# The opening of a fused block on one core: Pool makes the first two weight remainders, root and first tiles in PSUM, high-part products first, one more column product on VectorE

## The chip, the cores and the metric

One core of a Trainium2 chip runs the program; seven are idle. The metric is the device time of one execution in microseconds (us). The engines have names of two kinds: TensorE (PE in the profile; PEld is its weight load), VectorE (DVE), ScalarE (ACT), GpSimd (POOL, "Pool" in the text) and SyncE (SP), which here only issues DMAs.

## The reference, cut to what matters

The program computes a state-space mixer block with its MLP and then a gated linear attention block with its MLP, 512 tokens of 1024 features. Only the first lines of the first block are of concern here:

```
c_act = silu(c)
mod = (c_act @ w_ada + b_ada)            # shift1, scale1: 2 x 1024 of its values come first
u = rms_norm(x, ln1) * (1.0 + scale1) + shift1
proj = u @ w_in                          # dt columns, then B, C, xs, z ... of eight groups
dt = softplus(dt + dt_bias)
```

All of it is fp32. The kernel gets fp32 accuracy from three fp32r products for each matmul: weights and data are split into a rounded high part and a remainder, and it sums high x high, high weight x low data, and low weight x high data.

## The kernel before, in words

**Layout.** Data is held transposed: features on 128 partitions, 512 tokens along a row, eight tiles j = 0 to 7 for 1024 features. A weight unit is 128 output columns for all 1024 features: a 128x1024 tile `wraw`, of which ScalarE makes the rounded `whi` (hi_part, L416) and VectorE or Pool the remainder `wlo` (lo_part, L436). There are two raw slots and four split slots. The weight of dt has tiles of its own: `dw`, `dwh`, `dwl`.

**The opening.** The first 60 us hold what has no work beside it.
1. SP issues, in this order (L2680 to L2712): the parameters, x, the modulation weights' slab 0 (8 pieces), dw, weight units 0 and 1, slab 1, then it waits for remainder 0 (semaphore w_split), issues unit 2, slab 2, waits for remainder 1, issues unit 3, slab 3, and so on.
2. ScalarE squares the tiles of x (L2812), TensorE sums them with a matrix of ones into PSUM bank 6, ScalarE makes the root in `nrs` (Ln L548, Exp L550), then rounds dw into dwh (L2816).
3. The modulation comes in four chunks c, each for two tiles of u. VectorE multiplies the rows of a slab with c_act and adds them up, one operation for each of KD[c] pieces k (`columns`, L2994 and L2996, the sum is kept in PSUM bank 5; the last goes to `macc`). TensorE adds the remaining pieces itself (`direct`, L3242: eight minus KD[c] pieces) and sums macc over the partitions (`reduced`, L3249). VectorE then makes mod and g1s for two tiles (`modulation`, L3006 and L3008).
4. For each tile j of u: x times root (`scaled_a`: VectorE for tiles 0 and 1, L2971; Pool for 2 to 7, L2735), the rounded uhi (`rounded_a`, VectorE L2977, for tiles 0 and 2; ScalarE L2824 for the others), the full value on ScalarE (L2825, into two turns of `nsq`), and the low part ulo = full - uhi on VectorE (`low_a`, L2982). Semaphore "hi" counts full tiles, "u" counts low parts.
5. TensorE does 5 outputs (dt and weight units 0 to 3, banks 4, 0, 1, 2, 3) by 8 tiles by 3 products = 120 products (`first_units`; lines 1348 to 1350, called through `part`). The products of tile k wait for low part k, and each new output waits for its remainder (dw_lo, w_split).

**What sets the order.** Nothing but the order written for each engine, and semaphores between them: every engine works through its own list, and a wait at the head of it holds all behind. VectorE's list of the opening, before, is: columns of chunk 0, scaling 0, modulation 0, rounding 0, scaling 1, low 0, remainder dwl (L3018), remainder of unit 0, low 1, columns of chunk 1 (6), one of chunk 2, modulation 1, rounding 2, one column, low 2, one column, low 3, five columns, two of chunk 3, modulation 2, two, low 4, one, low 5, two, modulation 3, low 6, low 7. Pool's is: remainder of unit 1, scaling 2 and 3, remainder 2, remainder 3, scaling 4 to 7.

After the opening TensorE goes on with unit 4 (L450 to L452), the transposes of dt (they wait for the dt chain on VectorE and ScalarE) and the rest of the 280 units.

## Time and profile before

| | |
|---|---|
| median of 3 runs | 1746.01 us (1745.83 to 1746.41) |
| the profiled execution: time, span | 1746.1 us, 1744.4 us |
| mean granted TensorE clock | 0.997 |
| PE busy | 1722.9 us, 99% |
| PEld busy | 1457.2 us, 84% |
| DVE busy | 1203.4 us, 69% |
| ACT busy | 828.9 us, 48% |
| POOL busy | 312.8 us, 18% |

Shares of busy time are over the whole span, and the opening is a thirtieth of it. There the timelines have to be read: each gives the start of an instruction from the first instruction of the program, its length, engine, line, operation, output and input, and in brackets how long its engine had been idle before it and what ended that. The time of a run is some 1.7 us longer than the span. Matmul starts are spaced closer than their lengths, since they are pipelined: the distance of starts is what counts.

### The profile page before, as it was taken

The page shows a single profiled execution, that of the slowest core. Times are in us where ns is not written, and L with a number is a line of the kernel's source. Part 1 is how long each engine was busy: PE and PEld are TensorE (multiplying, and loading weights), DVE is VectorE, ACT ScalarE, POOL GpSimd, SP SyncE. Part 2 cuts the span into 40 slices and gives each one's busy share as a digit, 9 for nine tenths or more (in the row PEclk, how much of TensorE's full clock was granted, in tenths as well). Part 3 has the DMA queues.
Part 4 walks back from the last instruction along what each step waited for, and adds up shares of the span by engine and source line. Part 5 has one row for each costly group of instructions (what it writes and reads, how often), then busy time and mean ns, then how long its engine had stood idle before and what let it go on. Part 6 is the DMA issues. An engine that isn't in the chain of part 4 may idle for free.

```text
span 1744.4 us, 26127 instructions
## 1 busy us (share of the span) xinstructions
PE 1722.9 (99%) x9074; PEld 1457.2 (84%) x9074; DVE 1203.4 (69%) x1678; ACT 828.9 (48%) x1273; POOL 312.8 (18%) x370
## 2 busy tenths in 40 slices
PE   7999999999999999999999999999999999999998
PEld 4888888888888888888888888889998888999997
DVE  6788777775356665589855665776656788667764
ACT  4666666665322222355313543665544474444443
POOL 2111111110011110002111125221110112222212
PEclk9999999999999999999999999999999999999999
DMA  9343333332545563326555563111122414223221
GB/s 336 107 127 115 121 121 121 116 114 73 181 133 192 192 192 121 109 97 214 184 192 179 192 219 114 60 50 49 42 71 70 140 46 154 97 98 106 100 72 50
DMA packets 76245, 221.12 MB, mean 127 GB/s; under 512 B 9328, under 2 KB 19952, under 8 KB 76144
## 3 DMA queue, kind: packets, MB, share of 16 engines
q1 hardware_dynamic: 56944, 160.43, 27.6%
q0 software_dynamic: 17632, 56.83, 10.6%
q10 hardware_dynamic: 1568, 2.52, 0.5%
q8 instruction: 62, 1.02, 0.2%
q14 instruction: 39, 0.32, 0.1%
HBM read 217.52 MB, written 2.23 MB: 126 GB/s over the span
## 4 chain that ended last, share of the span: by engine, by line
PE 87%; DVE 6%; issue 3%; DVEq 2%; ACT 1%; DMA 1%; ACTq 0%; POOLq 0%; POOL 0%; SPq 0%
PE bank L450 16%; PE bank L451 16%; PE bank L452 16%; PE bank L1348 3%; PE bank L2412 3%; PE bank L2413 3%; PE bank L1349 3%; PE bank L1350 3%; PE bank L2414 3%; PE bank L2366 2%; PE bank L2368 2%; PE bank L2367 2%; PE bank L1401 1%; PE bank L1400 1%; PE bank L1399 1%
## 5 line engine op out<-in xcount | busy, mean ns | idle before, releaser
L436 DVE TENSOR_TENSOR wlo<-wraw,whi 128x1024 fp32r<-128x1024 f32 x246 | 311.6, 1268 | 125.5 <-ACT whi L416 104.9
L416 ACT ACTIVATE whi<-wraw 128x1024 fp32r<-128x1024 f32 x217 | 229.2, 1058 | 331.3 <-PE bank L452 216.2
L450 PE MATMUL bank<-uhi,whi 128*128 128x512 f32 x916 | 359.1, 392 | 0.2 <-DVE wlo L436 0.2
L452 PE MATMUL bank<-uhi,wlo 128*128 128x512 f32 x916 | 356.6, 389 | 0.0
L451 PE MATMUL bank<-ulo,whi 128*128 128x512 f32 x916 | 356.5, 389 | 0.0
L452 PEld LDWEIGHTS bank<-uhi,wlo 128*128 128x128 f32 x916 | 172.0, 188 | 36.1
L450 PEld LDWEIGHTS bank<-uhi,whi 128*128 128x128 f32 x916 | 172.0, 188 | 35.7 <-DVE wlo L436 0.6
L451 PEld LDWEIGHTS bank<-ulo,whi 128*128 128x128 f32 x916 | 172.0, 188 | 34.8
L1085 POOL DMA_DIRECT2D aring<-in_ada x160 | 86.0, 538 | 519.3 <-DVE aacc L1099 214.0
L450 PE MATMUL bank<-vhi,whi 128*128 128x512 f32 x408 | 159.5, 391 | 0.0
L452 PE MATMUL bank<-vhi,wlo 128*128 128x512 f32 x408 | 158.8, 389 | 0.0
L451 PE MATMUL bank<-vlo,whi 128*128 128x512 f32 x408 | 158.8, 389 | 0.0
L1099 DVE SCALAR_TENSOR_TENSOR aacc<-aring,c_act,aacc 128x512 f32 (+1 forms) x168 | 123.6, 750 | 11.4 <-issue 2.0
L2213 DVE TENSOR_TENSOR qlo<-qsrc,qhi 128x512 fp32r<-128x512 f32 x98 | 85.1, 890 | 45.4 <-ACT qhi L2207 33.3
L2412 PE MATMUL bank<-v2hi,whi 128*128 128x512 f32 x236 | 92.6, 392 | 0.0
L2413 PE MATMUL bank<-v2lo,whi 128*128 128x512 f32 x236 | 92.5, 392 | 0.0
L2414 PE MATMUL bank<-v2hi,wlo 128*128 128x512 f32 x236 | 91.8, 389 | 0.0
L450 PEld LDWEIGHTS bank<-vhi,whi 128*128 128x128 f32 x408 | 76.6, 188 | 16.3 <-DVE vlo L1212 0.3
L452 PEld LDWEIGHTS bank<-vhi,wlo 128*128 128x128 f32 x408 | 76.6, 188 | 16.0
L451 PEld LDWEIGHTS bank<-vlo,whi 128*128 128x128 f32 x408 | 76.6, 188 | 15.7
L1348 PE MATMUL bank<-uhi,whi 128*128 128x512 f32 x216 | 88.3, 409 | 0.0
L1350 PE MATMUL bank<-uhi,wlo 128*128 128x512 f32 x216 | 84.7, 392 | 0.0
(527 smaller groups left out, 3506.1 us busy)
## 6 DMA issues: line engine op xcount, KB each, us to landing
wraw<-in_units SPq DMA_DIRECT2D x252, 512.0 KB, 3.8
aring<-in_ada POOLq DMA_DIRECT2D x160, 256.0 KB, 3.5
qsrc<-in_units SPq DMA_DIRECT2D x28, 512.0 KB, 3.8
slab<-in_ada SPq DMA_DIRECT2D x32, 256.0 KB, 7.5
es<-decay_rows POOLq DMA_DIRECT2D x32, 256.0 KB, 4.6
eac<-decay_rows POOLq DMA_DIRECT2D x32, 128.0 KB, 2.9
x<-in_xT SPq DMA_DIRECT2D x4, 512.0 KB, 5.6
xr<-in_xT ACTq DMA_DIRECT2D x1, 2048.0 KB, 14.1
```

What stands on the lines that cost most here:

```text
L416: act.activation(whi[:, at % SLOTS, :], wraw[:, at % RAW, :], ACT.Copy).then_inc(w_hi, 1)
L436: dve.tensor_tensor(wlo[:, at % SLOTS, :], wraw[:, at % RAW, :], whi[:, at % SLOTS, :].bitcast(f32), ALU.subtract).then_inc(w_split, 1)
L450: pe.matmul(out, wh, rhs_hi(k), start=first and k == 0, stop=False)
L451: pe.matmul(out, wh, rhs_lo(k), start=False, stop=False)
L452: mm = pe.matmul(out, wl, rhs_hi(k), start=False, stop=last and k == KT - 1)
L1085: pool.dma_start(aring[:, n % ARING, :], src[k * P:(k + 1) * P, bass.ds(it * 512 + col0, 512)]).then_inc(N2[f"ada_ld{n % ARING}"], 16)
L1099: last = dve.scalar_tensor_tensor(acc, w, c, acc, ALU.mult, ALU.add)
L1348: pe.matmul(out, wh, rhs_hi(k), start=k == 0, stop=False)
L1350: mm = pe.matmul(out, wl, rhs_hi(k), start=False, stop=k == KT - 1)
L2412: pe.matmul(psum[i][:], whi[:, slot, s], v2hi[:, v + t, :], start=t == 0, stop=False)
L2413: pe.matmul(psum[i][:], whi[:, slot, s], v2lo[:, v + t, :], start=False, stop=False)
L2414: mm = pe.matmul(psum[i][:], wlo[:, slot, s], v2hi[:, v + t, :], start=False, stop=t == 3)
```

## The change: what it does

- **Pool** makes dwl and the remainders of units 0 and 1, ahead of its scalings; before, VectorE made the first two. Semaphores dw_hi and dw_lo become one, dw_split (1: dwh is there, 2: dwl too). Pool's scalings now also wait for dt_nega, which stands behind a second Exp.
- **Root in PSUM.** Ln goes to nrs, Exp to PSUM bank 6, from which VectorE scales tiles 0 and 1. Later, behind the copy of unit 1, ScalarE does the Exp once more, into nrs, for Pool's scalings.
- **Full tiles 0 and 1 in PSUM.** `full_a` gives banks 3 and 2, which units 3 and 2 use later; the other tiles stay in nsq.
- **KD** goes from [7, 6, 8, 7] to [7, 7, 8, 7]: chunk 1 has seven column products on VectorE and one piece on TensorE.
- **VectorE's order** of column products among low parts and modulations is another.
- **TensorE's order.** The first products wait for dwh and the rounded tile 0 (new semaphore u_first) and go out kind by kind: high x high, high weight x low data, remainder last. From tile 3 on the high and remainder products of a tile wait for the full tile ("hi"), and only the product with the low part waits for "u". `direct(1)` and `reduced(1)` come before anything of unit 2, `reduced(2)` among the products of unit 3, `reduced(3)` behind the first six products of tile 5.

```diff
-KD = [7, 6, 8, 7]
+KD = [7, 7, 8, 7]
...
+        def full_a(j):
+            return psum[3 - j][:] if j < 2 else nsq[:, j % 2, :]
...
-            pool.wait_ge(norm_sem["rs"], 1)
+            pool.wait_ge(S["dw_split"], 1)
+            pool.tensor_tensor(dwl[:], dw[:], dwh[:].bitcast(f32), ALU.subtract).then_inc(S["dw_split"], 1)
+            lo_part(pool, 0, 0)
+            lo_part(pool, 1, 0)
+            pool.wait_ge(S["dt_nega"], 1)
             pool.wait_ge(norm_sem["t"], 2)
-            pool.wait_ge(w_split, 1)
-            lo_part(pool, 1, 0)
             scaled_a(2)
             scaled_a(3)
             lo_part(pool, 2, 0)
...
-            norm_a.root(act, norm_a.bank)
+            act.activation(nrs[:], psum[6][:], ACT.Ln, scale=1.0 / D, bias=eps)
+            act.drain()
+            act.activation(psum[6][:], nrs[:], ACT.Exp, scale=-0.5).then_inc(norm_sem["rs"], 1)
             act.wait_ge(S["dw_ld"], 16)
-            act.activation(dwh[:], dw[:], ACT.Copy).then_inc(S["dw_hi"], 1)
+            act.activation(dwh[:], dw[:], ACT.Copy).then_inc(S["dw_split"], 1)
...
-                act.activation(nsq[:, j % 2, :], x0[:, j, :], ACT.Identity, scale=g1s[:, j:j + 1], bias=mod[:, j:j + 1]
+                act.activation(full_a(j), x0[:, j, :], ACT.Identity, scale=g1s[:, j:j + 1], bias=mod[:, j:j + 1]
                                ).then_inc(norm_sem["hi"], 1)
...
             hi_part(act, 1, 0)
+            act.activation(nrs[:], nrs[:], ACT.Exp, scale=-0.5)
             act.activation(nega[:], pc("a_log"), ACT.Exp).then_inc(S["dt_nega"], 1)
...
-                dve.tensor_tensor(x0[:, j, :], x0[:, j, :], nrs[:], ALU.mult).then_inc(norm_sem["t"], 1)
+                dve.tensor_tensor(x0[:, j, :], x0[:, j, :], psum[6][:], ALU.mult).then_inc(norm_sem["t"], 1)
...
-                dve.tensor_scalar(uhi[:, j, :], x0[:, j, :], g1s[:, j:j + 1], mod[:, j:j + 1], ALU.mult, ALU.add)
+                rounded = dve.tensor_scalar(uhi[:, j, :], x0[:, j, :], g1s[:, j:j + 1], mod[:, j:j + 1], ALU.mult, ALU.add)
+                if j == 0:
+                    rounded.then_inc(S["u_first"], 1)
...
-                dve.tensor_tensor(ulo[:, j, :], nsq[:, j % 2, :], uhi[:, j, :].bitcast(f32), ALU.subtract
+                dve.tensor_tensor(ulo[:, j, :], full_a(j), uhi[:, j, :].bitcast(f32), ALU.subtract
...
             low_a(0)
-            dve.wait_ge(S["dw_hi"], 1)
-            dve.tensor_tensor(dwl[:], dw[:], dwh[:].bitcast(f32), ALU.subtract).then_inc(S["dw_lo"], 1)
-            lo_part(dve, 0, 0)
+            columns(1, 0, 2)
             low_a(1)
-            columns(1, 0, KD[1])
-            columns(2, 0, 1)
+            columns(1, 2, KD[1])
             modulation(1)
             rounded_a(2)
-            columns(2, 1, 2)
             low_a(2)
-            columns(2, 2, 3)
+            columns(2, 0, 2)
             low_a(3)
-            columns(2, 3, KD[2])
-            columns(3, 0, 2)
+            columns(2, 2, KD[2])
+            columns(3, 0, 1)
             modulation(2)
-            columns(3, 2, 4)
+            columns(3, 1, 3)
             low_a(4)
-            columns(3, 4, 5)
+            columns(3, 3, 4)
             low_a(5)
-            columns(3, 5, KD[3])
+            columns(3, 4, KD[3])
...
+            def first_units(which, k):
+                pe.wait_ge(norm_sem["hi"], k + 1)
+                for n in which:
+                    product(n, k, "hi")
+                    product(n, k, "rest")
+                norm_a.ready(pe, k + 1)
+                for n in which:
+                    mm = product(n, k, "low")
...
+            pe.wait_ge(S["dw_split"], 1)
+            pe.wait_ge(S["u_first"], 1)
+            product(0, 0, "hi")
+            pe.wait_ge(w_hi, 1)
+            product(1, 0, "hi")
+            norm_a.ready(pe, 1)
+            products((0, 1), (0,), ("low",))
+            pe.wait_ge(norm_sem["hi"], 2)
+            products((0, 1), (1,), ("hi",))
+            pe.wait_ge(S["dw_split"], 2)
+            products((0,), (0, 1), ("rest",))
+            norm_a.ready(pe, 2)
+            products((0, 1), (1,), ("low",))
             pe.wait_ge(w_split, 1)
+            products((1,), (0, 1), ("rest",))
+            pe.wait_ge(w_hi, 2)
+            products((2,), (0, 1), ("hi", "low"))
             pe.wait_ge(w_split, 2)
+            products((2,), (0, 1), ("rest",))
             direct(1)
             reduced(1)
+            pe.wait_ge(w_hi, 3)
+            products((3,), (0, 1), ("hi", "low"))
+            norm_a.ready(pe, 3)
+            products((0, 1, 2), (2,), ("hi", "low", "rest"))
...
```

## Rows read from the trace of the kernel before

**Rows 1.** The page's chain that ended last: shares of the span by engine.
```profile
PE 87%; DVE 6%; issue 3%; DVEq 2%; ACT 1%; DMA 1%; ACTq 0%; POOLq 0%; POOL 0%; SPq 0%
```

**Rows 2.** Waits of TensorE, whole span: engine, line, releaser: total, times, longest.
```profile
PE bank L1348 <- DVE dwl L3018: 4.0, 1, 4.0
PE bank L1348 <- DVE ulo L2982: 1.2, 2, 0.6
```

**Rows 3.** Timeline of TensorE, opening: start, length, what, [idle before, releaser].
```profile
18.18 1.05 PE L3249 MATMUL bank<-con,macc 128*128 128x1 f32 x8
...
23.18 0.80 PE L1348 MATMUL bank<-uhi,dwh 128*128 128x512 f32 x1 [3.95 <-DVE dwl L3018]
...
28.44 1.84 PE L3242 MATMUL bank<-c_act,slab 128*128 128x1 f32 x16
30.14 1.03 PE L3249 MATMUL bank<-con,macc 128*128 128x1 f32 x8
...
34.22 0.50 PE L1348 MATMUL bank<-uhi,dwh 128*128 128x512 f32 x1 [0.60 <-DVE ulo L2982]
...
44.20 0.50 PE L1348 MATMUL bank<-uhi,dwh 128*128 128x512 f32 x1 [0.58 <-DVE ulo L2982]
...
47.74 0.95 PE L3242 MATMUL bank<-c_act,slab 128*128 128x1 f32 x8
...
59.79 0.39 PE L450 MATMUL bank<-uhi,whi 128*128 128x512 f32 x1
```

**Rows 4.** Timeline of VectorE, opening.
```profile
20.08 0.55 DVE L2977 TENSOR_SCALAR uhi<-x,g1s,mod 128x512 fp32r<-128x512 f32 x1
...
21.91 1.22 DVE L3018 TENSOR_TENSOR dwl<-dw,dwh 128x1024 fp32r<-128x1024 f32 x1
...
25.80 3.24 DVE L2996 SCALAR_TENSOR_TENSOR bank<-slab,c_act,bank 128x512 f32<-128x512 f32 x4
...
31.21 0.16 DVE L3006 TENSOR_TENSOR mod<-bank,par 128x4 f32<-128x4 f32 x1 [0.40 <-PE bank L3249]
31.45 0.47 DVE L3008 SCALAR_TENSOR_TENSOR g1s<-mod,par 128x2 f32<-128x2 f32 x1
...
41.33 0.16 DVE L3006 TENSOR_TENSOR mod<-bank,par 128x4 f32<-128x4 f32 x1
...
43.45 0.69 DVE L2982 TENSOR_TENSOR ulo<-nsq,uhi 128x512 fp32r<-128x512 f32 x1
...
44.89 1.17 DVE L2982 TENSOR_TENSOR ulo<-nsq,uhi 128x512 fp32r<-128x512 f32 x1
```

**Rows 5.** Timeline of ScalarE, opening.
```profile
18.85 1.04 ACT L2816 ACTIVATE dwh<-dw 128x1024 fp32r<-128x1024 f32 x1
...
23.10 1.04 ACT L416 ACTIVATE whi<-wraw 128x1024 fp32r<-128x1024 f32 x1
...
28.13 1.06 ACT L416 ACTIVATE whi<-wraw 128x1024 fp32r<-128x1024 f32 x1 [3.90 <-DMA wraw<-in_units]
...
42.62 0.80 ACT L2825 ACTIVATE nsq<-x,mod,g1s 128x512 f32<-128x512 f32 x1
```

**Rows 6.** Timeline of Pool, opening.
```profile
24.50 2.60 POOL L436 TENSOR_TENSOR wlo<-wraw,whi 128x1024 fp32r<-128x1024 f32 x1 [23.52 <-DVE wlo L436]
27.06 2.53 POOL L2735 TENSOR_TENSOR x<-x,nrs 128x512 f32<-128x512 f32 x2
29.54 2.37 POOL L436 TENSOR_TENSOR wlo<-wraw,whi 128x1024 fp32r<-128x1024 f32 x1
...
44.23 2.99 POOL L2735 TENSOR_TENSOR x<-x,nrs 128x512 f32<-128x512 f32 x2 [2.38 <-DVE ulo L2982]
```

**Rows 7.** Line 1534, VectorE copies beside Pool's products: ns min/median/max.
```profile
L1534 DVE COPY kdf<-ez x8: 294/673/1221, 1149.8 to 1272.7; 128x256 f32<-128x256 f32 x8
```

**Rows 8.** Timeline of SP's queue, opening.
```profile
24.29 0.34 SPq L2700 DMA_DIRECT2D wraw<-in_units  x1
```

**Rows 9.** Windows: stretch, busy of PE, PEld, DVE, ACT, POOL, granted clock, DMA.
```profile
20.00:22.00 2.00, 0.00 (x0) 0.00 (x0) 1.84 (x4) 1.98 (x3) 0.00 (x0) 0.50 1.09 351
...
26.00:28.00 2.00, 2.00 (x9) 1.57 (x8) 1.85 (x3) 0.00 (x0) 2.00 (x2) 0.79 1.00 354
```

51 lines of the change are left out of this document (27 added, 24 removed).

## The prediction, made before the change was timed

> **What bounds the kernel now.** I read the chain of waits first [rows 1]: 87% of it is TensorE, so the whole kernel ends when TensorE has done its matmuls. The waits of TensorE [rows 2] say where it is held up in the part that the change touches: 4.0 us for the first remainder (dwl), 1.2 us in two waits for the low parts of u. Then I put the timelines of the first 60 us side by side: TensorE [rows 3], VectorE [rows 4], ScalarE [rows 5], Pool [rows 6]. The reader is to see there that TensorE's first product starts at 23.18, that it waits again before 34.22 (u of tile 2) and before 44.20 (u of tile 4), and that from 44.20 it has no gap to 59.79, when the five opening accumulations are done. From 44.20 it does 60 products and two short stretches: 15 products in 47.74 - 44.20 = 3.54, so 0.236 each with restart, about 0.2275 in the flow. Nothing after 59.79 waits for long (the other waits of [rows 2] are elsewhere and small), so a shift of 59.79 goes into the end one to one. VectorE is the engine that sets 34.22 and 44.20: it is almost without idle time from 20 to 47, and the low parts stand between its column products.
>
> **The change, part by part.** The sum is made on the profiled execution: span 1744.4, its own time 1746.1, against a median of 1746.0; so a shift of the span is put straight on 1746.0.
>
> *Root and two full tiles in PSUM.* The Ln and Exp of the root and ScalarE's full tiles keep their length (0.80 to 0.81 a tile in [rows 5]; no row writes a 128x512 tile to PSUM, bounds 0.7 to 0.85; I take 0.80). ScalarE gets one more Exp (0.63 before, same row kind) after the second weight copy, in a stretch where it waits for a DMA until 28.13 [rows 5]: nothing. VectorE's two scalings and two subtractions take one operand from PSUM; the nearest rows are 0.69 and 0.75, I take 0.69.
>
> *Remainders to Pool.* VectorE loses dwl and wlo0: 1.22 each [rows 4], 2.3 us of its time at their spacing. Pool takes 2.37 for such an operation undisturbed [rows 6]. It starts when ScalarE has written dwh, 18.85 + 1.04 = 19.89 [rows 5], plus 0.08 to 0.17 (Pool starts 0.09 after the low part that ends at 44.14): 19.97 to 20.06. VectorE's rounding of tile 0 starts at 20.08 [rows 4]. This is the step on which I stake most. Pool and VectorE exclude each other for operations that use two SBUF reads: the g1s operation took 0.47 at 31.45 and ended with Pool's remainder (29.54 + 2.37 = 31.91), though the same form takes 0.16; the low part at 44.89 took 1.17 in place of 0.69 while Pool scaled [rows 4, 6]. Column products, with one operand in PSUM, ran beside Pool at full speed (3.24 for four from 25.80, with Pool busy since 24.50). The rounding reads one SBUF tensor, but takes 0.55 for 512 elements where a column product takes 0.75, so it seems to read by both ways, and a COPY with one SBUF source shows 0.29 at best and 0.67 in the median of eight, next to Pool's products [rows 7]. If it is excluded, it waits from 20.08 to about 0.15 before Pool's end at 22.34, and ends at 22.74 instead of 20.63. Bounds: 0 to 2.3 us; I take 2.1.
>
> On that point the Trainium skill is sharper than the rows. Its page "SBUF — State Buffer", section "SBUF: two separate sides", has the pair of ports shared by VectorE and GpSimd as an exclusive lock, for VectorE operations with two SBUF inputs or in a two-port mode; "VectorE: DVE Perf Modes", section "The perf-mode tier table (the rule you actually need)", puts an fp32 tensor_scalar from SBUF in such a mode. By these rules the rounding is held and the sum is the one below; without them for one-source operations it would be about 0 to +0.6. No row of this trace shows a TENSOR_SCALAR held by Pool.
>
> *What follows, in time.* PE: first product at 22.8 (before 23.18). Second scaling to 23.5, low part 0 to 24.1 (before 22.0). ScalarE waits for the scaling: uhi1, full tile 1 to 25.04, second weight copy to 26.0 (before 24.14 [rows 5]). Pool: wlo0 behind the rounding, 22.32 + 0.27 + 2.37 = 24.96; wlo1 26.08 to 28.45 (before 24.50 + 2.60 = 27.10 [rows 6]); tiles 2 and 3 scaled to 30.9 (2.53 for two; before 29.6); wlo2 30.9 to 33.26 (before 31.91). SP issues the third weight tile when wlo0 is written: at 24.98, before 24.29 [rows 8]; it landed 3.8 later and does so again, and all slabs behind it come 0.7 later. That is hidden: wlo2 waits for Pool, not for the tile, and the second slab is not read before 34.7.
>
> *KD 6 to 7 and the new places of column products.* One more product on VectorE, 0.83 at its spacing; TensorE's direct stretch halves, from 1.84 to 0.95 (its forms at 28.44 and 47.74 [rows 3]). Columns of chunk 1 now run from 24.0 to 30.45, with low part 1 between: 7 x 0.83 + 0.61. Before they ended at 29.9 (25.80 + 3.24, and one of 0.83 behind). TensorE: 18 products for outputs 0 to 2 by 29.2, direct 0.82 beside it, reduction 30.5 to 31.56, modulation(1) at 31.60 (before 31.21). g1s at 31.84 then waits for wlo2 until 33.2, rounding 2 at 33.4 (before right behind 31.92), low part 2 34.13 to 34.82 (before just ahead of 34.22). So u of tile 2 comes at 34.88 for TensorE, 0.66 late. VectorE's idle and held time here (1.1 before 31.60, 1.4 behind Pool) eats what it was relieved of; and of chunk 2 nothing is done, where two products had been done by then and a third was next.
>
> *Chunk 2 and 3.* From 34.7: two products, low part 3, six products, one of chunk 3: 9 x 0.83 + 0.7 = 8.2, to 43.0. modulation(2) at 43.14 (before 41.33 [rows 4]): 1.8 late. ScalarE's full tile 4 is written at 45.08 (before 42.62 + 0.80 = 43.42 [rows 5]).
>
> *High-part products first.* Before, tile 4 waited for its low part (44.14, start 44.20 [rows 3]). Now it starts on the full tile alone: 45.14. Of the 1.8 us the order gives back 0.8. TensorE has done its 38 other products, 38 x 0.2275 + 0.9 after 34.88, at 44.6 or so, so it waits 0.4 to 0.6 at that place as before. Tiles 5 to 7 have slack or lose about 0.15 (full tile 6 at 53.87 against TensorE at 53.8). Their 60 products and the two stretches are the same work: 45.14 + 15.6 + 0.15 = 60.9, against 59.79.
>
> The dt chain starts 1.5 later too, and TensorE gets to its transposes 1.1 later; before, it had about 1 us of slack there. Nothing is added.
>
> Sum: the end of the opening 1.1 us later, **1747.1**.
>
> **The rivals.**
> *A. VectorE gets in first at 20.08, or its rounding is not held.* For it: the two starts are only 0.02 to 0.11 apart. Then the first product is at 20.7, wlo0 25.2, wlo1 27.6, modulation(1) at 30.2. But the third tile lands at 29.0, its copy is ready at 30.1, and wlo2 starts at 30.3: g1s (30.4) is held to 32.5. u of tile 2 at 34.3, full tile 4 at 44.5: +0.5, 1746.5.
> *B. No operation of the opening is held twice* (Pool starts wlo2 after 30.7, or takes turns differently): low part 2 at 32.1, two us earlier than before, full tile 4 at 42.44, TensorE starts on it at 42.5 instead of 44.20, plus 0.2 lost in the thinner slack: -1.5, 1744.5. Against it: the held g1s and low part of [rows 4].
> *C. The clock falls again.* Slower than before: TensorE's clock was at the lower of its two levels (1.2 GHz, 0.50 in [rows 9]) from 20.0 to 26.8 after TensorE had only one-column matmuls (the last at 18.18 + 1.05 [rows 3]) and then none; it came back with TensorE busy since 23.18. In the forecast TensorE is idle from 32.4 to 34.9, in rival A from 31.1 to 34.3. Before, its gap there was 0.6. If this drops the clock for another 6.8 us while products are due, TensorE does half of what it would in them: 6.8 / 2 = 3.4 lost, less 0.6 of wait before tile 4: +2.8 on top, 1749.9. [...] Against it: the earlier fall followed a longer near-idle stretch.
> *D. The change does less than it says:* TensorE's early products, on half clock, win nothing because remainders and low part 2 end last anyway. That is inside the forecast and A.
>
> **How the numbers follow.** Forecast 0.45, A 0.25, B 0.13, C 0.12, other 0.05. The range has to reach B (1744.5) and most of C: 1744.2 to 1749.6; the likeliest's own range is 1746.3 to 1748.2 (the 0.15 and 0.08 us of each handover add up). A measurement of this kernel tells 0.2% from nothing, 3.5 us: faster than 1742.5 needs more than the stalls ahead of 34 and 44 (1.2) and the start won (2.5) without any loss, 0.03; slower than 1749.5 is half of C and a little, 0.07; within, 0.90.
>
> **What would show it.** Right: in the new timeline the rounding of tile 0 has some 2.6 us instead of 0.55 and ends 0.4 to 0.6 behind Pool's first remainder; g1s of chunk 1 is long and ends with Pool's wlo2; TensorE waits 2 to 3 us before the third output's tile 2 (34 to 35) and starts tile 4 at about 45. Wrong: a rounding of 0.55 beside a busy Pool; low part 2 before 33; TensorE free of gaps after 31; a granted clock of 0.50 after 30 (then C).

## The result and the profile after

The changed kernel takes **1748.71 us** (median of 22 runs, 1747.32 to 1750.33); the kernel before, on the same chips, 1746.32 (22 runs, 1745.13 to 1747.63). The ratio is 1.0014 [1.0009, 1.002]: 2.4 us slower, less than the 0.2% that the prediction took as no change, yet on the slower side of zero with its whole interval. The sign that was forecast is there, and so is the mechanism, on a neighbouring operation; +1.1 us was too little.

The profiled execution after has 1747.71 us, span 1746.0, mean clock 0.996. It is the third shortest of its kernel's 22: +1.6 against the profiled execution before, where the medians are +2.4 apart. The other 0.8 us can't be seen in this profile; only the times of the runs speak of them.

VectorE after, the lines that answer to [rows 4]:

```profile
19.69 2.28 DVE L3020 SCALAR_TENSOR_TENSOR g1s<-mod,par 128x2 f32<-128x2 f32 x1
22.07 0.55 DVE L2987 TENSOR_SCALAR uhi<-x,g1s,mod 128x512 fp32r<-128x512 f32 x1
...
32.39 0.16 DVE L3018 TENSOR_TENSOR mod<-bank,par 128x4 f32<-128x4 f32 x1 [1.97 <-PE bank L3257]
32.63 0.85 DVE L3020 SCALAR_TENSOR_TENSOR g1s<-mod,par 128x2 f32<-128x2 f32 x1
...
34.37 0.69 DVE L2994 TENSOR_TENSOR ulo<-nsq,uhi 128x512 fp32r<-128x512 f32 x1 [0.24 <-ACT nsq L2834]
...
43.46 0.16 DVE L3018 TENSOR_TENSOR mod<-bank,par 128x4 f32<-128x4 f32 x1 [0.29 <-PE bank L3257]
43.70 0.37 DVE L3020 SCALAR_TENSOR_TENSOR g1s<-mod,par 128x2 f32<-128x2 f32 x1
```

Pool after, for [rows 6]:

```profile
19.62 2.34 POOL L2741 TENSOR_TENSOR dwl<-dw,dwh 128x1024 fp32r<-128x1024 f32 x1 [18.64 <-ACT dwh L2825]
23.85 4.73 POOL L436 TENSOR_TENSOR wlo<-wraw,whi 128x1024 fp32r<-128x1024 f32 x2 [1.89 <-ACT whi L416]
28.54 2.52 POOL L2738 TENSOR_TENSOR x<-x,nrs 128x512 f32<-128x512 f32 x2
31.10 2.37 POOL L436 TENSOR_TENSOR wlo<-wraw,whi 128x1024 fp32r<-128x1024 f32 x1
...
41.52 2.54 POOL L2738 TENSOR_TENSOR x<-x,nrs 128x512 f32<-128x512 f32 x2
```

Pool's dwl runs from 19.62 to 21.96. In it stands an operation on two numbers a partition, g1s, that takes 0.16 us elsewhere: 2.28 us, to 21.97. The rounding behind it has its usual 0.55. The same again at 32.63, where g1s ends with Pool's remainder of unit 2 (31.10 + 2.37 = 33.47, g1s 33.48). A short one follows in chunk 2: g1s takes 0.37 at 43.70 and ends with Pool's scalings (41.52 + 2.54 = 44.06).

TensorE after, for [rows 3], and SP's queue, for [rows 8]:

```profile
22.76 0.77 PE L3268 MATMUL bank<-uhi,dwh 128*128 128x512 f32 x1 [3.35 <-DVE uhi L2987]
23.82 0.80 PE L3268 MATMUL bank<-uhi,whi 128*128 128x512 f32 x1 [0.30 <-ACT whi L416]
...
27.07 0.63 PE L3268 MATMUL bank<-ulo,dwh 128*128 128x512 f32 x1
27.50 0.63 PE L3268 MATMUL bank<-ulo,whi 128*128 128x512 f32 x1
...
31.32 1.03 PE L3257 MATMUL bank<-con,macc 128*128 128x1 f32 x8
...
35.12 0.50 PE L3268 MATMUL bank<-uhi,dwh 128*128 128x512 f32 x1 [1.73 <-DVE ulo L2994]
...
45.68 0.50 PE L3268 MATMUL bank<-uhi,dwh 128*128 128x512 f32 x1 [0.32 <-ACT nsq L2834]
...
61.55 0.39 PE L450 MATMUL bank<-uhi,whi 128*128 128x512 f32 x1
```

```profile
26.26 0.34 SPq L2703 DMA_DIRECT2D wraw<-in_units  x1
```

The opening ends at 61.55 instead of 59.79, +1.76, and the span is 1.6 longer. In this pair of executions what the opening loses arrives at the end; that it does so to a few tenths is not a rule, as the note below the table of the experiments shows. The waits of TensorE [rows 2] are now 3.4 us in one for the rounded tile 0 and 1.7 in one for low part 2.

The windows after, columns as in [rows 9]; the granted clock is the third number from the end:

```profile
20.00:22.00 2.00, 0.00 (x0) 0.00 (x0) 1.97 (x1) 0.00 (x0) 1.96 (x1) 0.50 1.09 353
...
26.00:28.00 2.00, 2.00 (x6) 1.51 (x6) 1.87 (x3) 0.74 (x3) 2.00 (x2) 0.50 0.42 113
28.00:30.00 2.00, 2.00 (x7) 1.61 (x6) 1.83 (x3) 0.04 (x1) 2.00 (x3) 0.61 0.91 312
30.00:32.00 2.00, 2.00 (x18) 1.88 (x17) 0.42 (x1) 1.02 (x1) 1.97 (x2) 1.00 0.98 331
```

The granted clock has two levels, 1.2 and 2.4 GHz (0.50 and 1.00). So a window of 2 us at 0.79 [rows 9] has 0.84 us at the lower one, and one at 0.61 has 1.56: the clock came back at 26.8 before and at 29.6 after. Until then products start 0.43 apart instead of 0.23 (27.07 to 27.50 above). From 26 to 28 TensorE has six records, where before it had nine. DMA has a hole there, 113 GB/s against 354: SP's queue has issued nothing since 20.4 and issues the third weight tile only at 26.26, behind the late remainder 0.

### The profile page after: what moved, and what is told of

The parts are those of the page before. It is cut to its first block, busy times and chain, and to the rows that moved or that the text cites. A ratio compares the mean times of both kernels' runs of the same rounds, so it can differ in the third digit from the quotient of the medians.

```text
span 1746.0 us, 26109 instructions
## 1 busy us (share of the span) xinstructions
PE 1723.7 (99%) x9066; PEld 1456.4 (83%) x9066; DVE 1204.1 (69%) x1677; ACT 829.5 (48%) x1274; POOL 316.5 (18%) x372
## 4 chain that ended last, share of the span: by engine, by line
PE 85%; DVE 6%; issue 3%; DVEq 2%; ACT 2%; DMA 1%; ACTq 0%; SPq 0%; POOLq 0%; POOL 0%
PE bank L450 16%; PE bank L452 16%; PE bank L451 16%; PE bank L2412 3%; PE bank L2413 3%; PE bank L2414 3%; PE bank L1348 2%; PE bank L1350 2%; PE bank L1349 2%; PE bank L2366 2%; PE bank L2368 2%; PE bank L2367 2%; PE bank L1401 1%; PE bank L1399 1%; PE bank L1400 1%
## 5 line engine op out<-in xcount | busy, mean ns | idle before, releaser
L450 PE MATMUL bank<-uhi,whi 128*128 128x512 f32 x916 | 359.1, 392 | 0.2 <-DVE wlo L436 0.2
L452 PE MATMUL bank<-uhi,wlo 128*128 128x512 f32 x916 | 356.6, 389 | 0.0
L1348 PE MATMUL bank<-uhi,whi 128*128 128x512 f32 x184 | 75.3, 409 | 0.0
L1350 PE MATMUL bank<-uhi,wlo 128*128 128x512 f32 x184 | 71.9, 391 | 0.0
```

What stands on the lines that cost most here:

```text
L450: pe.matmul(out, wh, rhs_hi(k), start=first and k == 0, stop=False)
L452: mm = pe.matmul(out, wl, rhs_hi(k), start=False, stop=last and k == KT - 1)
L1348: pe.matmul(out, wh, rhs_hi(k), start=k == 0, stop=False)
L1350: mm = pe.matmul(out, wl, rhs_hi(k), start=False, stop=k == KT - 1)
```

## The experiments

Each of the twelve kernels was run 11 times, the changed kernel 22 times, in turns with the kernel before on the same chip. *After* means the changed kernel. A "filler" is an extra matmul of dwh with itself into a bank whose content nobody reads; it leaves the output as it is.

| kernel | median | before | difference | ratio [95%] | opening ends* |
|---|---|---|---|---|---|
| after | 1748.71 | 1746.32 | +2.39 | 1.0014 [1.0009, 1.002] | 61.55 |
| 1 dwl behind rounding 0 | 1747.49 | 1745.90 | +1.59 | 1.0008 [0.9999, 1.0017] | 62.66 |
| 2 and wlo2 behind rounding 2 | 1747.86 | 1745.90 | +1.96 | 1.0011 [1.0002, 1.002] | 62.61 |
| 3 dwl, wlo0 on VectorE again | 1747.62 | 1745.90 | +1.72 | 1.0011 [1.0002, 1.002] | 60.45 |
| 4 after with fillers | 1746.77 | 1745.90 | +0.87 | 1.0002 [0.9993, 1.0011] | 61.57 |
| 5 no hold up to low part 2, fillers | 1746.14 | 1746.10 | +0.04 | 1.0001 [0.9992, 1.001] | 60.89 |
| 6 before with fillers | 1745.78 | 1746.10 | -0.32 | 1.0 [0.9991, 1.0009] | 60.23 |
| 7 as 3, fillers | 1746.53 | 1746.10 | +0.43 | 1.0004 [0.9995, 1.0013] | 59.98 |
| 8 as 4, KD[1] = 6 | 1747.61 | 1746.10 | +1.51 | 1.001 [1.0001, 1.0019] | 63.64 |
| 9 as 5, slabs loaded ahead | 1748.88 | 1746.68 | +2.20 | 1.0011 [1.0002, 1.002] | 61.98 |
| 10 as 9, two products ahead | 1748.46 | 1746.68 | +1.78 | 1.0012 [1.0003, 1.0021] | 61.76 |
| 11 before, high part first | 1746.51 | 1746.68 | -0.17 | 0.9999 [0.999, 1.0008] | 59.31 |
| 12 unit 0 first on Pool | 1745.45 | 1745.99 | -0.54 | 0.9997 [0.9988, 1.0006] | 59.05 |

*In the one profiled execution, whose time may lie up to 1.8 us off the median: the profiled ones of 5 and 8 are 0.9 and 1.7 above theirs, that of 3 is 1.8 below. Intervals are some 1.6 us wide to each side (1 us for the changed kernel's), so differences under that are read as hints, and the timelines carry the argument. The ratio is not the quotient of the two medians; for kernel 4 it stands for 0.3 us where the medians are 0.87 apart.

Three more things have to be known before single executions are compared.
- *They do not start alike.* The first modulation on VectorE starts at 19.59 before and 19.45 after, but at 19.94 in kernel 1, 19.84 in kernel 5, 18.98 in kernel 11 and 19.11 in kernel 12. The column "opening ends" holds these shifts of up to 0.6 us.
- *They do not end alike.* From the end of the opening to the end of the span it is 1684.6 us before and 1684.5 after, but 1683.5 in kernel 2 and 1685.5 in kernel 11. No opening explains that; it is as large as the whole effect, and its cause is open.
- *The clock.* In these profiles the lower level lasts, summed over the opening, 6.8 us before and in kernels 3 and 6, 10.2 in the changed kernel and in 1, 2, 8 and 11, 3.4 in 4, 7, 9 and 10, and nothing in 5 and 12. Behind the opening all have 1.00 up to the last few microseconds.

**1. Pool's dwl starts behind the rounding of tile 0.**

```diff
             pool.wait_ge(S["dw_split"], 1)
+            pool.wait_ge(S["u_first"], 1)
             pool.tensor_tensor(dwl[:], dw[:], dwh[:].bitcast(f32), ALU.subtract).then_inc(S["dw_split"], 1)
```

> The changed kernel, but Pool's first remainder also waits until VectorE has rounded tile 0 (so it starts some 0.9 us later and holds nothing of modulation 0). Before is 1746.3, the changed kernel 1748.7. Ports theory (Pool's remainders hold VectorE's modulation of chunks 0 and 1, each for 1 to 2 us, and that carries the loss): the g1s operation of chunk 0 falls from 2.28 to 0.16 us, the first product starts at about 20.6 instead of 22.76, the second hold stays or grows to 2 us because wlo2 now starts about when modulation 1 is ready; the end of the opening 0.8 to 1.3 us earlier than in the changed kernel, total 1747.4 to 1748.0. Clock theory (the time goes to TensorE's products at the lower clock level): the lower clock lasts as long as before or longer, since the products are even thinner spread; total 1748.5 to 1749.5. Order theory (it is VectorE's list, not the holds): within 0.5 of the changed kernel.

VectorE, then TensorE behind it, and two windows, in this kernel:

```profile
20.18 0.16 DVE L3021 SCALAR_TENSOR_TENSOR g1s<-mod,par 128x2 f32<-128x2 f32 x1
20.44 0.55 DVE L2988 TENSOR_SCALAR uhi<-x,g1s,mod 128x512 fp32r<-128x512 f32 x1
...
30.96 2.07 DVE L3021 SCALAR_TENSOR_TENSOR g1s<-mod,par 128x2 f32<-128x2 f32 x1
```

```profile
34.65 0.80 PE L3269 MATMUL bank<-uhi,dwh 128*128 128x512 f32 x1 [2.82 <-DVE ulo L2995]
```

```profile
32.00:34.00 2.00, 0.00 (x0) 0.00 (x0) 1.66 (x3) 0.94 (x2) 1.01 (x1) 0.65 1.06 367
34.00:36.00 2.00, 1.35 (x3) 1.17 (x4) 1.83 (x3) 1.28 (x2) 0.00 (x0) 0.50 1.07 384
```

The first hold is gone (g1s 0.16) and TensorE starts at 21.13 instead of 22.76. Everything reaches chunk 1 some 1.7 us earlier, and there g1s runs into Pool's remainder 2 with its full length: 2.07 us. TensorE waits 2.82 for low part 2, its clock falls to 0.50 in that gap, and the products of tile 2 run at half speed to 39.4. That is rival C of the prediction, seen directly. The opening ends 1.1 later than that of the changed kernel, 0.5 of it by this execution's later start; the median is still 0.8 nearer to the kernel before than the changed kernel's is.

**2. Also the remainder of unit 2 behind the rounding of tile 2.**

```diff
             pool.wait_ge(S["dw_split"], 1)
+            pool.wait_ge(S["u_first"], 1)
             pool.tensor_tensor(dwl[:], dw[:], dwh[:].bitcast(f32), ALU.subtract).then_inc(S["dw_split"], 1)
...
             scaled_a(3)
+            pool.wait_ge(S["u_first"], 2)
             lo_part(pool, 2, 0)
...
-                if j == 0:
+                if j in (0, 2):
                     rounded.then_inc(S["u_first"], 1)
```

> As the run before, and Pool's remainder of unit 2 also waits until VectorE has rounded tile 2, so that neither modulation 0 nor 1 is held by a remainder. Ports theory: low part 2 is ready at about 32 instead of 35.1, tile 4 starts 2 us earlier, total 1744.5 to 1746.0, that is at or below before (1746.3): the whole loss and more is the two holds. Clock theory: the same time as the run before, 1748.5 or more. Order theory: 1747.5 to 1748.5, since VectorE's order leaves it idle ahead of modulation 1.

Pool and VectorE:

```profile
31.54 2.35 POOL L436 TENSOR_TENSOR wlo<-wraw,whi 128x1024 fp32r<-128x1024 f32 x1 [1.16 <-DVE uhi L2989]
```

```profile
31.70 2.73 DVE L2996 TENSOR_TENSOR ulo<-nsq,uhi 128x512 fp32r<-128x512 f32 x1 [0.24 <-ACT nsq L2836]
```

The hold only moves to the next operation with two SBUF inputs: low part 2 takes 2.73 instead of 0.69, and TensorE waits 2.96 at the same place, with the same fall of its clock. The gain that was expected of taking both holds away did not come, since none was taken away. To take a hold away, Pool has to stand behind the last such operation of the chain, not behind one of them.

**3. dwl and remainder 0 back on VectorE, all else as after.**

```diff
-            pool.wait_ge(S["dw_split"], 1)
-            pool.tensor_tensor(dwl[:], dw[:], dwh[:].bitcast(f32), ALU.subtract).then_inc(S["dw_split"], 1)
-            lo_part(pool, 0, 0)
+            pool.wait_ge(w_split, 1)
             lo_part(pool, 1, 0)
...
             low_a(0)
+            dve.wait_ge(S["dw_split"], 1)
+            dve.tensor_tensor(dwl[:], dw[:], dwh[:].bitcast(f32), ALU.subtract).then_inc(S["dw_split"], 1)
+            lo_part(dve, 0, 0)
             columns(1, 0, 2)
```

> The changed kernel, but VectorE makes the first two remainders again, at their old place behind low part 0, and Pool begins with the remainder of unit 1; all else of the change stays (root and tiles in PSUM, order of TensorE, column products). Ports theory: no hold of modulation 0, VectorE 2.3 us busier ahead of chunk 1, so modulation 1 is 1 us later than it could be, but not held by more than 0.5; total 1746.5 to 1748.0. Clock theory: first product at 20.6 but waits for the remainders as before; 1746.3 to 1747. Order theory: 1748.7 or more, since VectorE has one product more and both remainders: plus 0.8 on before from the product alone, plus 0.8 from the order of chunk 2.

```profile
32.00:34.00 2.00, 1.76 (x4) 0.84 (x4) 1.55 (x4) 1.52 (x3) 0.03 (x1) 0.51 1.09 384
34.00:36.00 2.00, 1.93 (x6) 1.56 (x7) 1.76 (x4) 0.71 (x1) 0.00 (x0) 0.63 1.03 373
```

No g1s is long in this kernel (0.16 at 32.28), yet the median stays at +1.7. The windows above show a second fall of the clock (0.51 and 0.63), although the wait for low part 2 is only 0.31 here. Its eleven runs fall into two groups: six with a mean clock of 0.996 to 0.997 take 1745.35 to 1747.62 us, five with 0.994 to 0.995 take 1748.96 to 1749.78. A mean clock lower by 0.001 over 1746 us is 3.5 us more at the lower level, up to 1.7 us of products. So the clock looks like a cause of its own, and it differs between executions of one kernel. The changed kernel shows the same: its eight runs at 0.995 have a mean of 1749.7, the fourteen others lie between 1747.3 and 1749.0. No execution at 0.995 or below was profiled (kernel 3's profile is one of the fast group, 1745.85), so where in these executions the clock is low is not shown.

**4. The changed kernel with fillers** where TensorE waits: six ahead of the first product, six ahead of low part 2.

```diff
             pe.wait_ge(S["dw_split"], 1)
+            for _ in range(6):
+                pe.matmul(psum[4][:], dwh[:, 0:P], dwh[:, 0:T], start=True, stop=True)
             pe.wait_ge(S["u_first"], 1)
...
             products((3,), (0, 1), ("hi", "low"))
+            for _ in range(6):
+                pe.matmul(psum[6][:], dwh[:, 0:P], dwh[:, 0:T], start=True, stop=True)
             norm_a.ready(pe, 3)
```

> The changed kernel with 12 more matmuls whose results nobody reads: 6 while TensorE waits for the first rounded tile (19.6 to 22.7), 6 while it waits for low part 2 (33.4 to 35.1). They keep TensorE busy in the two gaps. Clock theory: the clock comes back some us earlier than 29.5 and does not fall a second time in any execution, the mean clock is 0.997 or above in all, and the time falls by 1.0 to 1.5 to 1747.3 or less, with the spread of the runs (3.0 us) cut to 1.5. Ports theory: at most 0.3 us faster, since TensorE waits for low part 2 in any case; spread unchanged.

```profile
31.82 0.16 DVE L3018 TENSOR_TENSOR mod<-bank,par 128x4 f32<-128x4 f32 x1 [1.34 <-PE bank L3257]
32.06 1.71 DVE L3020 SCALAR_TENSOR_TENSOR g1s<-mod,par 128x2 f32<-128x2 f32 x1
```

```profile
35.40 0.50 PE L3268 MATMUL bank<-uhi,dwh 128*128 128x512 f32 x1 [1.20 <-DVE ulo L2994]
```

+0.87 instead of +2.39, both against the kernel before: by the medians about 1.5 of the 2.4 us go with the fillers. All eleven runs lie within 1746.15 and 1747.7, ten of them at 0.998 or more, so the high group is gone. Both holds are still there (g1s 2.02 and 1.71). Part of the lower level is not: the windows have 1.00 from 20 to 24 and 0.70, 0.50, 0.95 from 24 to 30.

The timelines do not show that gain. Modulation 1 comes 0.6 earlier than in the changed kernel (31.82 against 32.39), but g1s is then held until Pool's remainder 2 is done, and tile 2 (35.40 against 35.12) and the end of the opening (61.57 against 61.55) are no earlier. So in the changed kernel's profiled execution the first stay at the lower level costs next to nothing: the hold behind it hides it. The 1.5 us are a matter of executions that were not profiled.

**5. No hold up to low part 2, and fillers.** dwl waits for the rounding of tile 0, the remainder of unit 2 for low part 2; fillers in each gap of TensorE up to 33 us (22 matmuls in five places, not shown below).

```diff
             pool.wait_ge(S["dw_split"], 1)
+            pool.wait_ge(S["u_first"], 1)
             pool.tensor_tensor(dwl[:], dw[:], dwh[:].bitcast(f32), ALU.subtract).then_inc(S["dw_split"], 1)
...
             scaled_a(3)
+            norm_a.ready(pool, 3)
             lo_part(pool, 2, 0)
```

> Both causes taken out of the changed kernel: Pool's first remainder behind the rounding of tile 0, its remainder of unit 2 behind low part 2 (so neither modulation 0, modulation 1 nor low part 2 is held), and idle stretches of TensorE filled with matmuls that nobody reads (4, 6 of half width, 3, 3 and 6). Two-cost theory (holds and clock each cost 1 to 2 us, and taking one away alone calls up the other, as in the two runs with Pool behind the roundings, where the clock fell again at 32.6 us): low part 2 at about 31.8 to 32.3 against 34.9 in the changed kernel, clock at its upper level from 26 at the latest and no second fall, end of the opening at 58.5 to 59.5 (61.55), total 1744.0 to 1745.2. Clock-only theory: like the changed kernel with the fillers, 1746.3 to 1747. Holds-only theory: the fillers add nothing, 1747.4 as the runs before.

```profile
31.11 0.16 DVE L3022 SCALAR_TENSOR_TENSOR g1s<-mod,par 128x2 f32<-128x2 f32 x1
...
34.60 1.27 DVE L2996 TENSOR_TENSOR ulo<-nsq,uhi 128x512 fp32r<-128x512 f32 x1
...
41.59 0.76 DVE L3008 TENSOR_SCALAR bank<-slab,c_act 128x512 f32<-128x512 f32 x1 [0.91 <-DMA slab<-in_ada]
...
42.66 0.72 DVE L3022 SCALAR_TENSOR_TENSOR g1s<-mod,par 128x2 f32<-128x2 f32 x1
```

```profile
33.06 0.39 PE L3270 MATMUL bank<-uhi,dwh 128*128 128x512 f32 x1
...
45.03 0.50 PE L3270 MATMUL bank<-uhi,dwh 128*128 128x512 f32 x1 [1.29 <-ACT nsq L2836]
```

Level with the kernel before (+0.04, within 1.6), clock 1.00 in every window from 20 to 40. By the medians, holds and clock together are the whole loss. But taking both away wins nothing, where 1744.0 to 1745.2 was expected: tile 2 is 2.1 us earlier than in the changed kernel (33.06 against 35.12), tile 4 only 0.65 (45.03 against 45.68). Three things on VectorE eat the lead. At 41.59 it waits 0.91 for a slab: SP stood behind remainder 0, which Pool finished at 25.8 here (before: 24.3, [rows 8]), and every load behind it came later. And two operations behind low part 2 are held by Pool: low part 3 (1.27 for 0.69), beside the moved remainder 2, and g1s of chunk 2 (0.72 for 0.16), beside scalings.

**6. The kernel before with seven fillers** behind dwh, ahead of the wait for dwl.

```diff
+            pe.wait_ge(S["dw_hi"], 1)
+            for _ in range(7):
+                pe.matmul(psum[4][:], dwh[:, 0:P], dwh[:, 0:T], start=True, stop=True)
             pe.wait_ge(S["dw_lo"], 1)
             first_units((0,), (0,))
```

> The kernel before, with 7 matmuls that nobody reads between 19.9 and its first product at 23.2. Its 9 first products went at the lower clock (0.43 apart in place of 0.23), 1.8 us. Clock theory in the simple form (each product at the lower level costs its 0.2 us): 1744.2 to 1744.8. Two-cost theory: TensorE waits for low part 2 at 34.2 all the same, so this is worth 0.3 us at most, 1745.6 to 1746.0; the clock cost of the changed kernel is in a second fall and in products behind 35.

-0.32, not told from nothing. The clock stays at 1.00 from 20 to 24 and falls later instead (0.50 in 26 to 28, and again in 32 to 34), 6.8 us in sum as in the kernel before: here fillers in one gap moved the fall and did not remove it.

**7. Kernel 3 with fillers** in the three gaps of TensorE.

```diff
             pe.wait_ge(S["dw_split"], 1)
+            for _ in range(4):
+                pe.matmul(psum[4][:], dwh[:, 0:P], dwh[:, 0:T], start=True, stop=True)
             pe.wait_ge(S["u_first"], 1)
             product(0, 0, "hi")
+            for _ in range(6):
+                pe.matmul(psum[7][:, 0:256], dwh[:, 0:P], dwh[:, 0:256], start=True, stop=True)
...
```

Not shown: five more of 512 columns ahead of low part 1, and two ahead of low part 2.

> The run with the first two remainders back on VectorE, with fillers (4, 6 of half width, 5 and 2) in TensorE's idle stretches. That run had 11 executions from 1745.35 to 1749.78 in two groups: clock 0.996 to 0.997 up to 1747.6, clock 0.994 to 0.995 from 1749.0. Clock theory: the upper group goes, all executions at 0.997 or more, median 1745.0 to 1745.8, below before. If the spread has another cause: median stays at 1747 to 1748, spread above 3.

+0.43 instead of +1.72; ten of eleven runs at or below 1747.0 and at 0.998 or more, one at 0.997 with 1748.99. The high group of kernel 3 is gone but for that one, which speaks for the clock. With VectorE making the remainders the rest of the change is level too, within 1.6 us: no gain of it is seen that the transfer to Pool could have destroyed. (1745.0 to 1745.8 was expected.)

**8. Kernel 4 with six column products in chunk 1.**

```diff
-KD = [7, 7, 8, 7]
+KD = [7, 6, 8, 7]
```

> The changed kernel with its 12 fillers (1746.8, 0.9 above before) but KD[1] = 6: one column product less on VectorE, eight more one-column matmuls on TensorE. Holds theory: modulation 1 is held by Pool's remainder in any case and the product runs in time that VectorE has, so no change beyond 0.3 us, or slower by TensorE's 0.8: 1746.8 to 1747.6. Order theory (VectorE's own work bounds it): 0.8 faster, 1746.0.

+1.51 against +0.87, inside each other's intervals. In the profiled execution, the slowest of the eleven, the clock is at 0.51, 0.50 and 0.50 from 32 to 38 in spite of the fillers, and the opening ends 2.1 later than in kernel 4. So neither a gain nor a loss by the seventh product is shown.

**9. Kernel 5 with slab 1 and half of slabs 2 and 3 issued before SP's waits.**

```diff
-            def modulation_columns(c):
+            def modulation_columns(c, k0=0, k1=KT):
...
+            modulation_columns(1)
             for u in range(RAW, 2 * RAW):
-                modulation_columns(u - RAW + 1)
+                modulation_columns(u, 0, 4)
                 sp.wait_ge(w_split, u - RAW + 1)
                 sp.dma_start(wraw[:, u % RAW, :], units[u]).then_inc(w_loaded[u % RAW], 16)
-            modulation_columns(3)
+                modulation_columns(u, 4, KT)
```

> The run with the holds off and the gaps filled (1746.1, level with before), and SP issues the first half of slabs 2 and 3 ahead of its waits for the remainders of units 0 and 1 instead of behind them. In that run the third weight tile was issued at 25.8 (24.3 in before) and the loads behind it came 1.3 to 2.8 us later than in before; VectorE waited 0.9 us for slab 3. Queue theory (what is left of the loss is the loads, which SP holds until Pool's later remainders are written): slab 3 begins to land before 40, modulation 2 some 1.0 us earlier, tile 4 at 44.0 instead of 45.0, total 1745.0 to 1745.4. Rival (VectorE's own list from low part 2 on bounds tile 4, the load is hidden): 1745.8 to 1746.3.

```profile
31.02 1.06 ACT L416 ACTIVATE whi<-wraw 128x1024 fp32r<-128x1024 f32 x1 [6.46 <-DMA wraw<-in_units]
```

```profile
32.13 0.80 PE L3271 MATMUL bank<-uhi,whi 128*128 128x512 f32 x1 [1.80 <-ACT whi L416]
```

A miss: +2.2. The DMA engines are full (shares of 1.06 to 1.11 in every window from 20 to 34), so what goes ahead pushes something back: the copy of the third weight tile starts at 31.02 (29.34 in kernel 5, 29.96 in the changed one), and TensorE waits 1.80 for its high part. Its clock falls there too (0.52 from 32 to 34).

**10. Kernel 9 with two products of chunk 2 ahead of modulation 1,** in VectorE's idle time.

```diff
             columns(1, 2, KD[1])
+            columns(2, 0, 2)
             modulation(1)
             rounded_a(2)
             low_a(2)
-            columns(2, 0, 2)
```

> The run before, and VectorE does two column products of chunk 2 ahead of modulation 1, where it is idle for 1.8 us, instead of behind low part 2. Order theory (VectorE's list from low part 2 to modulation 2 sets tile 4): modulation 2 comes 1.5 us earlier, tile 4 at 42.5 to 43.5, total 1743.8 to 1744.6, below before. Rival (slab 2 is not there by 29 and the products push modulation 1 back): 1745.5 to 1746.5.

+1.78, no better than 9 within the intervals: the weight tile is late all the same, and low part 3 falls into Pool's remainder 2 (2.31 us at 34.37). Five of its eleven runs are above 1749, four of them at a clock of 0.997 to 0.999, so a low clock is not what makes its high times; what does is open.

**11. The kernel before with high-part and remainder products first** from tile 3 on.

```diff
+                    if k >= 3 and len(which) > 1:
+                        pe.wait_ge(norm_sem["hi"], k + 1)
+                        for n in which:
+                            out, hi, lo = outs[n]
+                            pe.matmul(out[:], hi[:, k * P:(k + 1) * P], u_h(k), start=False, stop=False)
+                            pe.matmul(out[:], lo[:, k * P:(k + 1) * P], u_h(k), start=False, stop=False)
+                        norm_a.ready(pe, k + 1)
+                        for n in which:
+                            out, hi, lo = outs[n]
+                            mm = pe.matmul(out[:], hi[:, k * P:(k + 1) * P], u_l(k), start=False, stop=k == KT - 1)
...
```

> The kernel before with one part of the change only: from tile 3 on the high x high and remainder products of all outputs go ahead of the ones with the low part, and wait for the full tile alone. The prediction gave this part 0.8 us at tile 4. If TensorE's wait of 0.6 us ahead of tile 4 is all there is to win, it starts 0.6 earlier there and the total is 0.4 to 0.6 below before (1745.6); if tiles 6 and 7 then lose it again, 0 to 0.2.

-0.17, where 0.4 to 0.6 less was one expectation and 0 to 0.2 less the other. The order costs or brings nothing that can be told within 1.6 us. In the profile the wait of 0.58 ahead of tile 4 is gone (TensorE gets there at 43.86 without a gap), but it is late itself, as the granted clock was 0.73 and 0.50 in 30 to 34, in a kernel that has TensorE as busy as the one before.

**12. Unit 0 first.** Pool makes the remainders of units 0 and 1, scales tiles 2 and 3, and only behind low part 2 makes the remainder of unit 2 and dwl. TensorE does dt's remainder products behind tile 3 of the other outputs. Fillers in the gaps.

```diff
-            pool.tensor_tensor(dwl[:], dw[:], dwh[:].bitcast(f32), ALU.subtract).then_inc(S["dw_split"], 1)
             lo_part(pool, 0, 0)
             lo_part(pool, 1, 0)
...
             scaled_a(3)
+            norm_a.ready(pool, 3)
             lo_part(pool, 2, 0)
+            pool.wait_ge(S["dw_split"], 1)
+            pool.tensor_tensor(dwl[:], dw[:], dwh[:].bitcast(f32), ALU.subtract).then_inc(S["dw_split"], 1)
...
-            first_units(range(4), 3)
+            first_units((1, 2, 3), 3)
+            pe.wait_ge(S["dw_split"], 2)
+            products((0,), (0, 1, 2), ("rest",))
+            first_units((0,), 3)
```

> A version built on the earlier runs: Pool makes the remainder of unit 0 first (as early as VectorE did in before, so SP's queue is released at 24.4 and not at 26.3), then unit 1, the scalings of tiles 2 and 3, and behind low part 2 the remainders of unit 2 and of dt (dwl); TensorE takes dt's three remainder products only behind tile 3 of the other outputs; 15 matmuls that nobody reads fill its gaps. Nothing of modulation 0, modulation 1 or low part 2 is held. If the loss of the change was in three places, the holds, the clock, and the loads held back by the late remainder 0, this has none of them: low part 2 at 31.6 (34.2 in before), third weight tile landed by 28.5, full tile 4 at 42.5 (43.4), the end of the opening at 58.0 to 58.8 (59.8), total 1744.3 to 1745.2 with before at 1746 to 1746.7, so ratio 0.9990 to 0.9995. If the late loads are no cost (the runs with slabs ahead only lost by their late weight tiles for another reason): as the run with the holds off and gaps filled, ratio 1.0000.

```profile
29.75 0.16 DVE L3021 SCALAR_TENSOR_TENSOR g1s<-mod,par 128x2 f32<-128x2 f32 x1
```

```profile
31.54 0.50 PE L3269 MATMUL bank<-uhi,dwh 128*128 128x512 f32 x1 [0.36 <-DVE ulo L2995]
...
43.22 0.50 PE L3269 MATMUL bank<-uhi,dwh 128*128 128x512 f32 x1 [0.84 <-ACT nsq L2835]
...
59.05 0.39 PE L450 MATMUL bank<-uhi,whi 128*128 128x512 f32 x1
```

```profile
23.80 0.34 SPq L2703 DMA_DIRECT2D wraw<-in_units  x1
```

Remainder 0 is ready at 23.8, SP is released as early as in the kernel before, no operation up to tile 2 is held, the clock is 1.00 in every window from 20 to 40. Against kernel 5 tile 4 comes 1.8 us earlier; 0.7 of that is the earlier start of this execution, and 1.1 is left for the loads, the order of Pool and dt's late products together. Low part 3 and g1s of chunk 2 are held here too (1.27 at 33.24, 0.89 at 40.72). This is the fastest of all kernels, 2.9 us under the changed one by the differences, with -0.54 against the kernel before; but its ratio, 0.9997 [0.9988, 1.0006], does not show it faster, and 1744.3 to 1745.2 was expected of it. Of the 0.74 by which its opening ends before that of the kernel before, 0.48 is its execution's: its first modulation starts that much sooner.

## Why the prediction came out as it did

**The hold of the first remainder: right in mechanism and size, one operation off.** The prediction had Pool start at 19.97 to 20.06 and catch the rounding at 20.08. Pool started at 19.62, since the root and the rounding of dwh came 0.35 earlier, and caught g1s at 19.69 for 2.1 us more than its 0.16. Kernels 4 and 8, which leave Pool's order as it is, have the same (2.02 and 2.05). The first product at 22.76 is where it was forecast (22.8). That is luck in part: the hold has the same length on either operation, and a hold of g1s delays the rounding behind it just as much. The prediction looked at the operation that stood nearest to Pool's start, and not at the one ahead of it, a quarter of a microsecond away:

```profile
19.82 0.16 DVE L3008 SCALAR_TENSOR_TENSOR g1s<-mod,par 128x2 f32<-128x2 f32 x1
```

It did not give the same for ScalarE. Full tile 0 needs g1s, and the copy of unit 0 stands behind it in ScalarE's list; with g1s late the copy ran at 22.73 (before 20.74), and Pool, idle for 1.89, began remainder 0 only at 23.85; it was done at about 26.2, where the forecast had 24.96.

**What was staked on an operation with one source.** The rounding has 0.55 in every timeline, but it never stood beside a running remainder, so for it no run decides. The trace of the kernel before does decide it for a copy from SBUF to SBUF. The prediction gave the copies of line 1534 only as a minimum and a median [rows 7]. One by one, three of the eight take 0.29; the other five take 0.66 to 1.22, and Pool is at work at the start of each of these:

```profile
1183.32 1.21 DVE L1534 COPY kdf<-ez 128x256 f32<-128x256 f32 x1
...
1223.77 0.29 DVE L1534 COPY kdf<-ez 128x256 f32<-128x256 f32 x1
```

```profile
1182.67 1.71 POOL L1544 TENSOR_TENSOR ki<-ki,kf 128x512 f32<-128x512 f32 x1 [0.24 <-issue]
```

Pool's product ends at 1184.38 and the copy at 1184.53. So this copy, with one SBUF source and an SBUF output, is held as well. The first column product of a chunk, with one SBUF source and its output in PSUM, is not (0.75 at 24.09 in the changed kernel, beside Pool's remainder 0). The traces agree with the sharper rule of the Trainium skill ("SBUF — State Buffer", "SBUF: two separate sides": an exclusive lock for the whole instruction, whoever starts first), for two SBUF inputs with 2.28, 2.07 and 2.73 us, and for a copy with this 1.21.

**The second hold: right.** g1s 0.85 (forecast: 31.84 to 33.2), TensorE at tile 2 at 35.12 (34.88).

**The load: "0.7 later, hidden" was too little.** SP issued the third tile at 26.26, 2.0 later than before, since Pool makes remainder 0 behind dwl at 2.4 us each and behind the copy at 22.73. The tile was hidden, but barely: its copy ended at 31.02 and Pool's scalings at 31.06; in kernel 4 Pool waits 0.24 for it. The slabs behind it were hidden in the changed kernel, where no operation waits for one, and no longer once the holds were gone (kernel 5).

**The clock within the profiled execution: mis-sized, and hidden.** The forecast let products run fast from about 26.8 as before and set modulation(1) at 31.60; rival C was for a second fall only. In fact the first stay at the lower level was longer, to 29.6: between 26.8 and 29.6 seven products or so, at 0.43 instead of 0.23, cost up to 1.3 us of TensorE, and the reduction that modulation(1) waits for ended accordingly late: 32.39, +0.8. Kernel 4 shows that this is not what set tile 2: there modulation(1) is at 31.82, and the hold by Pool's remainder 2 hides the difference.

**Where the profiled execution's +1.76 instead of +1.1 is.** 0.24 stand at tile 2, since Pool's remainder 2 ends at 33.47 and not at 33.26; 0.3 more at tile 4 (45.68, forecast 45.14), mostly the third hold, g1s at 43.70, that the forecast did not have; 0.1 in the products behind it. Together they are within the range that the forecast gave itself (1746.3 to 1748.2).

**The rest, from +1.6 to +2.4, is the term that the sum did not have: the clock of other executions.** The forecast gave a further fall of the clock 0.12, as an either-or for all of them, with +2.8. The eight runs at a mean clock of 0.995 (mean 1749.68) are 1.4 us above the mean of the other fourteen (1748.23). Without the eight the median would be 1748.17, so they account for 0.5; fillers take back 1.5 in all. The sign that the prediction set for rival C, 0.50 after 30, is not in the changed kernel's profile; it is in those of kernels 1, 2, 3, 6, 8, 9 and 11. That the eight runs had it too is likely and not shown. Not all the spread is clock, either: among the fourteen, eight at 0.997 are even 0.7 above six at 0.996. What makes that is open. So is why the clock came back after different stays, in kernels whose TensorE was similarly busy.

**Rival A, the rounding gets in first, +0.5.** Kernel 1 is that rival made by a wait: first product 21.13 (20.7), g1s held to 33.03 (32.5), tile 2 at 34.65 (34.3). Up to there its account holds; the fall of the clock in the gap of 2.82, which its +0.5 does not contain, comes on top, and the median is +1.6.

**Rival B, nothing held, -1.5: no gain is seen.** Kernel 5 comes nearest to it, with the clock kept up as well, and is level. Its low part 2 is done at 32.85 (forecast 32.1), 1.3 us before that of the kernel before, but full tile 4, forecast for 42.44, was written only at 45.0. What it left out is the load behind the late remainder 0 (0.91) and the holds of low part 3 and of g1s in chunk 2 (0.58 and 0.56). Kernel 12, which gives unit 0 its place back, regains 1.1 us at tile 4 beyond its earlier start.

**High-part products first:** forecast to give back 0.8 at tile 4. There TensorE started on the full tile as forecast, at 45.68, while low part 4 ran from 45.66 to 46.35: it had 0.7 us of work in hand. Kernel 11 shows no gain at the end from this order alone, within 1.6 us; the 0.8 is neither shown nor excluded.

**The sum.** By the medians, of +2.4 about 1.5 go with the fillers of kernel 4 and 0.8 more with kernel 5, which takes the holds up to low part 2 away and has more fillers too. The intervals do not separate the two shares, and holds and clock are not independent: taking a hold away (kernel 1) opened a gap in which the clock fell. What the change takes off VectorE, two operations of 1.22, is given back in idle time ahead of modulation(1) (1.97 us at 32.39, 0.40 in [rows 4]): VectorE ceased to be what sets that point.

## What to carry to other kernels

Before an SBUF operation is given to GpSimd, list every VectorE operation with two SBUF inputs that may fall into its span, tiny ones on the critical chain above all, and put GpSimd behind the last of them. A copy from SBUF to SBUF belongs on the list too. A remainder that frees a load slot is also a link of the load chain: putting it first is what the fastest kernel did. A gap of TensorE at the start of a kernel costs its length and then, in some executions, a stretch at half speed. Unread matmuls in the gaps of the changed kernel cut that stretch from 10.2 us to 3.4 (kernel 4) or to nothing (5 and 12), but not reliably: kernel 8 has the same fillers as 4, and 10.2.

## What the runs showed of the hardware that was not expected

- A 128x2 operation is held as long as a large one: 2.28 us for 0.16 of work, as it started 0.07 behind Pool.
- TensorE's mean clock differs between executions of the same kernel; the time of kernel 3 splits with it into two groups 1.3 us apart at their nearest. Even the order of the kernel before, with the small edits of 6 and 11, has it at 0.50 in 32 to 34, where the profile before has 1.00.
- A hold does not need two sources: a copy of 128x256 from SBUF to SBUF took 1.21 instead of 0.29 beside Pool.
- The hold works in both directions. In kernel 12 low part 3 (from 33.24, 1.27 us) waited for Pool's remainder 2 (31.57 + 2.40 = 33.97) and ended at 34.51; Pool's dwl, begun at 33.92, took 2.85 instead of 2.34 to 2.40.
